# Which semaphore TensorE waits for between two levels of a gated scan

## The reference: two layers of a diffusion backbone

The input is 256 latent tokens and 256 context tokens of width 1024. The first layer mixes tokens by Fourier groups and spatial gates and ends in a dense SwiGLU. The second layer, which the change concerns, is a bidirectional gated linear recurrence (HGRN2) with 8 heads, followed by a top-2-of-8 expert SwiGLU. A final RMSNorm gives the output.

## Time and profile before

| | |
|---|---|
| median of the runs | 1965.93 us (1964.19 to 1966.01) |
| the profiled execution | 1965.33 us, span 1963.5 us |
| TensorE busy | 1810.3 us, 92% of the span |
| VectorE busy | 814.0 us, 41% |
| ScalarE busy | 685.7 us, 35% |
| the four scan groups | about 721 us to 1000 us of the span |

### The profile page before, as it was taken

How to read it: one execution, slowest core, us unless ns; L and a number is a source line. 1 busy time by engine, 2 the same in 40 slices (tenths; PEclk the granted TensorE clock), 3 DMA queues, 4 the chain that set the end, 5 groups by cost and what they waited for, 6 DMA issues and landing times.

```text
span 1963.5 us, 28385 instructions
## 1 busy us (share of the span) xinstructions
PE 1810.3 (92%) x11616; PEld 1333.3 (68%) x11616; DVE 814.0 (41%) x1174; ACT 685.7 (35%) x892; POOL 3.0 (0%) x6
## 2 busy tenths in 40 slices
PE   5899999999999889989878999999989899998987
PEld 2677676787687688889777787766546777763433
DVE  2532342333233455566637985554204444410002
ACT  3231432221223554355356764444003344400001
POOL 0000000000000000000000000000000000000000
PEclk8897999999999999999879999999999999999997
DMA  8642356434523122221128979999999999999993
GB/s 320 250 161 90 93 182 236 172 96 140 204 88 96 64 86 65 76 75 55 60 92 285 373 291 397 408 409 409 409 409 392 356 362 373 409 408 409 409 409 153
DMA packets 161701, 479.70 MB, mean 244 GB/s; under 512 B 14961, under 2 KB 58145, under 8 KB 155426
## 3 DMA queue, kind: packets, MB, share of 16 engines
q1 hardware_dynamic: 161570, 477.88, 64.6%
HBM read 476.77 MB, written 1.05 MB: 243 GB/s over the span
## 4 chain that ended last, share of the span: by engine, by line
PE 71%; DMA 13%; DVE 7%; ACT 4%; SPq 3%; issue 2%; DVEq 0%; ACTq 0%
PE ps L607 15%; PE ps L608 15%; PE ps L609 15%; PE ps L1328 5%; DMA arena<-in_moe_up 5%; DMA raw<-in_moe_up 4%; DMA arena<-in_moe_w 3%; PE ps L1399 3%; SPq L557 2%; PE ps L621 2%; DVE w_lo L1838 2%; PE ps L1317 2%; PE ps L637 1%; PE ps L1391 1%; PE ps L1149 1%
## 5 line engine op out<-in xcount | busy, mean ns | idle before, releaser
L1838 DVE TENSOR_TENSOR w_lo<-raw,w_hi 128x1024 fp32r<-128x1024 f32 x242 | 292.8, 1222 | 414.3 <-ACT w_hi L1468 411.7
L1468 ACT ACTIVATE w_hi<-raw 128x1024 fp32r<-128x1024 f32 x242 | 252.6, 1056 | 496.4 <-PE ps L609 381.3
L607 PE MATMUL ps<-h_hi,w_hi 128*128 128x512 f32 (+1 forms) x736 | 286.5, 389 | 18.9 <-DVE h_lo L1920 10.8
L608 PE MATMUL ps<-h_hi,w_lo 128*128 128x512 f32 (+1 forms) x736 | 278.0, 378 | 0.0
L609 PE MATMUL ps<-h_lo,w_hi 128*128 128x512 f32 (+1 forms) x736 | 277.5, 377 | 0.0
L1838 DVE TENSOR_TENSOR w_lo<-arena,w_hi 128x1024 fp32r<-128x1024 f32 x144 | 171.9, 1221 | 120.0 <-ACT w_hi L1468 117.5
L1468 ACT ACTIVATE w_hi<-arena 128x1024 fp32r<-128x1024 f32 x144 | 151.5, 1059 | 155.5 <-DMA arena<-in_moe_up 88.7
L607 PEld LDWEIGHTS ps<-h_hi,w_hi 128*128 128x128 f32 x736 | 142.6, 194 | 73.9 <-issue 47.3
L609 PEld LDWEIGHTS ps<-h_lo,w_hi 128*128 128x128 f32 x736 | 142.1, 193 | 25.7
L608 PEld LDWEIGHTS ps<-h_hi,w_lo 128*128 128x128 f32 x736 | 142.5, 194 | 23.3 <-issue 0.5
L607 PE MATMUL ps<-w_hi,s_hi 128*128 128x512 f32 x336 | 135.0, 402 | 3.0 <-DVE s_lo L2343 2.4
(11 more groups left out here) (345 smaller groups left out, 2301.0 us busy)
## 6 DMA issues: line engine op xcount, KB each, us to landing
arena<-in_moe_up SPq DMA_DIRECT2D x256, 512.0 KB, 9.8
raw<-in_moe_up SPq DMA_DIRECT2D x192, 512.0 KB, 10.0
arena<-in_moe_w SPq DMA_DIRECT2D x128, 512.0 KB, 11.7
raw<-in_moe_w SPq DMA_DIRECT2D x96, 512.0 KB, 11.3
raw<-in_ffn_w SPq DMA_DIRECT2D x66, 512.0 KB, 5.5
arena<-in_w_ada SPq DMA_DIRECT2D x32, 1024.0 KB, 5.0
raw<-in_w_in_odd SPq DMA_DIRECT2D x40, 512.0 KB, 3.5
scratch<-in_w_ada SPq DMA_DIRECT2D x16, 1024.0 KB, 5.5
```

What stands on the lines that cost most here:

```text
L607: pe.matmul(dst, s_h, m_h, start=start, stop=False, **kw)
L608: pe.matmul(dst, s_l, m_h, start=False, stop=False, **kw)
L1468: act.activation(w_hi[:, o % R, :], src, ACT.Copy).then_inc(hi_done, 1)
L1838: dve.tensor_tensor(w_lo[:, o % R, :], src, w_hi[:, o % R, :].bitcast(F32), ALU.subtract).then_inc(lo_done, 1)
```

```diff
@@ level, TensorE
                 else:
-                    pe.wait_ge(l_upd, len(LEVELS) * g + n)
+
+                    pe.wait_ge(l_wide, len(LEVELS) * g + n)
                     if n == 1:
 
                         pe.wait_ge(dg_out, g + 1)
@@ widen, VectorE
                 b, hs = base(g), LEVELS[n]
+                if n:
+
+                    dve.wait_ge(l_upd, len(LEVELS) * g + n)
                 dve.wait_ge(l_mm, len(LEVELS) * g + n + 1)
                 for at, (x, y) in ((R_LF, (R_KF, R_T + hs)), (R_LB, (R_T + G_LAT, R_KB + hs))):
```

## The result

| | before | after |
|---|---|---|
| median of 6 runs each | 1965.70 us | 1977.93 us |
| lowest to highest | 1964.19 to 1966.74 | 1973.09 to 1980.20 |
| profiled execution, span | 1965.33, 1963.5 us | 1973.09, 1971.1 us |
| mean granted clock of TensorE | 0.959 | 0.947 |

The ratio is 1.0055, with a 95% interval of 1.0041 to 1.0068: slower, by more than 0.2%, the least that can be told from no change, and outside the forecast range. The profiled execution is the fastest of the six after, so it shows 7.6 us of the 12.

A forecast was written before the change was run, and what follows sets the result against it. TensorE, busy for 92% of the span, was taken as the bound. Profiled 1965.33 us less 2.0 us from group 3, all other terms 0, gave 1963.3 us; plus 0.60 us for the median, 1963.9 us, range 1961.7 to 1966.4 us.

The forecast's parts named there:

- The instruction that is waited for, and the step at each wait: Level 1, group 3: TensorE waits for line 2128, about 1.4 us; level 6, groups 0 to 2: wait 0.8 us shorter.
- the second rival: Level 6, groups 0 to 2: cross and outputs move too, 2.4 us more gained, 1961.5 us; chance 7%.
- The added wait: 0: VectorE's 24 added waits, 6 in each group: taken as 0, upper end 0.66 us in the sum.
- I take the middle, 2.0 us: Levels 1 and 2 of group 3: level 2 starts 1.28 to 2.86 us earlier, taken as 2.0 us.
- a bound of 1.28 us below: Level 2 of group 3: least gain, with TensorE's pieces as slow as before, 4.85 us.
- costs TensorE directly: Group 3 behind level 1's wait: low clock less likely, but no longer mostly under VectorE's mask and totals.
- Value: 0 for each of the three: Waits ahead of level 6, groups 0 to 2: 0.8 us won each comes back as longer wait at the cross.
- a sign that it was wrong: Wrong if, among other signs, outputs of groups 0 to 2 start later at a clock below 1.
- The last rival: Groups 0 to 2: longer waits ahead of crosses lower the clock, 2.1 us per group, 1968.1 us with two; chance 6%.
- I let the 2.0 us through to the end.: Behind group 3's early levels: everything to the kernel's end, experts included, starts 2.0 us earlier.
- The page's rule: TensorE's idle gaps between matmul bursts lower the clock; trace agreed behind the 2.66 us gap, not ahead of crosses.
- The 1 us that the prediction gave to noise: Forecast range: medians add about 1 us on either side, from three runs of before spanning 1.8 us.

The follow-up runs named there:

- e1: Against the kernel before: only VectorE's added wait for its own totals kept, TensorE waits for the totals as before; 1966.99 us, ratio 1.0001.
- e2: Against the kernel before: TensorE waits for the widening in group 3 alone, VectorE's added wait stays; 1970.15 us, ratio 1.0019.
- e3: Against the kernel before: TensorE waits for the widening ahead of level 6 in groups 0 to 2 alone, VectorE's added wait stays; 1974.39 us, ratio 1.0036.
- e10: e3 with filling matmuls of constants, one ahead of level 6 and two ahead of the cross in groups 0 to 2; 1966.41 us, ratio 0.9995 to before.
- e7: The kernel before with one matmul of constants (0.9 us) added ahead of level 3 of group 3; 1974.21 us, ratio 1.0033.
- e8: The whole change with filling matmuls of constants in TensorE's waits in the scan and behind it; 1961.06 us, ratio 0.9964 to before.
- e11: The kernel before, waits as before, with all the filling of e8 but without the change; 1968.31 us, ratio 0.9998.
- e12: The kernel of e8 run again, on one chip with e11; 1960.56 us, ratio 0.9963 to before.
- e6: e2 with three matmuls of constants (2.7 us) added ahead of level 3 of group 3; 1970.07 us, ratio 1.0010 to before.
- e5: The kernel before, waits as before, with filling matmuls of constants in TensorE's waits in the scan only; 1968.14 us, ratio 1.0004.

## Why the prediction was wrong

- *The instruction that is waited for, and the step at each wait.* Right: 1.39 us at level 1 of group 3 ("about 1.4"), 0.78 us less at each level 6 ("0.8"), given back at the cross. VectorE widened level 6 no earlier, so the second rival falls.
- *The added wait: 0.* Right within the measurement (e1).
- *The gain in group 3: "I take the middle, 2.0 us".* Right in mechanism and size only where the clock held (2.7 us, e2). The sum had a bound of 1.28 us below, and this bound was wrong. It took level 1, the sum of squares and the transposes to last 4.85 us at worst, as they did before; they took 5.54 us, so level 2 came 0.6 us earlier and not 1.3. And it let nothing be lost behind level 2, while the low clock lasted 10.2 us and the group as a whole lost 1.7 us. I had written that where it falls now it "costs TensorE directly", and yet had not let it last longer.
- *"Value: 0 for each of the three" at level 6.* This step failed, and by itself it costs 7 us (e3), in its profiled execution about 1 us directly behind the crosses and the rest further on, most of it at the two gathers. The outputs of group 1 started later at a clock below 1, which the prediction had named as a sign that it was wrong. The last rival had named the mechanism, its place and its price for a group (in group 1 a low stretch of 6.8 us, the length that I had priced; it delayed the outputs by 0.9 us against the 2.1 us written, since part of it fell in the wait). I gave it 6%, because "after the waits at the cross of up to 3.0 us the clock was 1.00 in both groups". That was two samples at one alignment. The wait at the cross went from 3.0 to 3.75 us in group 1, the clock fell, and e10 shows that filled waits bring it back. The rival's own time, 1968.1 us, was 9.8 us short: it had no term for what comes behind the scan.
- *"I let the 2.0 us through to the end."* Failed, and no rival named it; in the profiled execution of after it is the larger part, 5.7 of 9.6 us. I took the work behind the scan to be rigid against a shift. The chain behind it is serial, and does move along, but its clock is not the same for each position: e7 pays 6.5 us for 0.9 us of work. That a gain can be lost behind the place where it was made, with nothing waiting for anything new, is not to be read from the waits, the chain or the timelines around the edit.
- *The page's rule.* Of the Trainium skill's advice against idle gaps between bursts of matmuls (TensorE: Matmul & The Clock Gate, Why this matters for your kernels) I had written that "by the page alone the last rival would be likelier than my 6%". The clock did fall there: the measured 0.50 behind the 3.75 us ahead of the cross of group 1 agrees with the page. The fall at the second gather is not covered by it, since TensorE was busy there without a gap.

What stays open: what in a shift decides (the low stretch at the second gather is in after, e2, e3, e7, e8, e11 and e12, and not in before and the other six), what lets the low clock of group 3 last 10.2 us in one kernel and 3.4 us in another, why the first gather was slow in e6 and not in e5 at nearly the same shift, and how the timed runs come to spread: those of after over 7 us, those of the kernel before, in the later comparisons, from 1959.7 to 1973.6 us over 34 runs. A part of the spread arises behind 1497 us of before, in code that no edit touches: there the profiled executions win up to 4.2 us on before or lose up to 4.4 us. The 1 us that the prediction gave to noise came from three runs and was too little. The profiles show one execution each, and the split into 3.9 and 5.7 us is the profiled run's, not that of the medians.

## What to carry to other kernels

Before moving a wait on TensorE, read the granted clock around it and behind it, and ask what the idle time does at its new place: a gap that cost nothing in the schedule was followed here by half the clock. In this kernel 0.9 us of added work cost 6.5 us, so a small edit should be judged with the clock held as far as it can be, by matmuls of constants in the waits on both sides of the comparison (e11 against e12), and not by its bare time. It also pays to compare the starts of the same instructions in both traces from end to end: that shows where a gain is lost. Filling is worth trying where the profile shows a wait with a clock under 1 behind it; it brought this change from 0.55% slower to 0.36% faster, while the same filling without the change brought nothing (0.9998).

## What the runs showed of the hardware

The granted clock fell from 2.4 to 1.2 GHz in the midst of a stretch in which TensorE was busy for the whole time: after 6 us of f32 gather matmuls with 128 and 64 columns (1143.6 to 1149.5 us in after). In the kernel before the same matmuls, which begin at 1140.0 us there, passed at 1.00. In the seven of the fourteen profiled executions that lost the clock there, it fell 5.8 to 7.3 us after the gather began. So a busy share of 100% in the profile did not keep the clock up here, and a stretch of small f32 matmuls is a place to look at.
